# Twelve more tiles of a Trainium2 kernel's first input projection as products of rounded halves, with another order of the column blocks

## The chip, the cores and the metric

The kernel runs on 1 core of one Trainium2 chip. The metric is device microseconds of one execution; lower is better. Engines are called TensorE (PE in the profile, PEld for its weight loads), VectorE (DVE), ScalarE (ACT), GpSimd (POOL) and SyncE (SP, which issues nearly all DMAs).

## What is computed

Two layers, one after the other. The first is a hybrid block: the normalised stream u (272 positions, 1024 channels) is projected to q, f, i, g (1024 columns each, for 8 HGRN heads), z (1024), x, B, C (1536 together, with a causal convolution) and dt, for a Mamba-2 mixer of 16 heads. Both mixers' outputs go through w_out, and a gated feed-forward with convolution follows. The second layer has a retention mixer and 16 experts. The change is in the first input projection, `proj = u @ w_in`:

```python
u = rmsnorm(h, norm1_w[l])
proj = u @ w_in[l]
hg_q, hg_f, hg_i, hg_g, m2_z, m2_xbc, m2_dt = jnp.split(proj, PROJ_SPLITS, axis=-1)
out_a = hgrn2_mixer(hg_q, hg_f, hg_i, hg_g, lbs[l], hg_norm_w[l])
out_b = mamba2_mixer(m2_z, m2_xbc, m2_dt, m2_conv_w[l], m2_conv_b[l], m2_dt_bias[l],
                     m2_a_log[l], m2_d[l], m2_norm_w[l])
h = h + jnp.concatenate([out_a, out_b], axis=-1) @ w_out[l]
...
def hgrn2_mixer(q, f_pre, i_in, g, lb, norm_w):
    f = lb + (1.0 - lb) * jax.nn.sigmoid(f_pre)
    k = 1.0 - f
    ...
    return (o * jax.nn.silu(g.astype(f32))).astype(q.dtype)
```

## The kernel before

**Tiles and units.** The projection has 52 tiles j = 0 to 51 (NPROJ, and one for dt), each 128 output columns by 272 positions over 8 blocks of 128 inputs. Four tiles share one unit of weights of 2 MB in a slot of `ring`. `ORDER` (L434) lists which block of 512 columns each unit holds: blocks 0 and 1 are q, 2 and 3 f, 4 and 5 i, 6 and 7 g, 8 and 9 z, 10 to 12 x, B and C. Tile j is column block ORDER[j // 4], part j % 4. Blocks 1, 3, 5 and 7 belong to HGRN heads 4 to 7.

**Two kinds of tile.** A tile outside `SPLIT` is 8 float32 products of `ring` and `uT` (L980). A tile in `SPLIT` (L53) is made of three products for each of the 8 blocks (`split_products`, L725, the products at L740, L741 and L744): ScalarE rounds the tile's weights into the last ring slot (`round_weights`, L1443, the operation at L1450), which holds four tiles (HB); VectorE subtracts the rounded from the full weights in place (`in_rest`, L1853, the operation at L1858, semaphore in_lo). TensorE waits for in_lo of its tile. The stream u has been rounded and split the same way once; `uin` (L244) says where the halves lie: in places of `proj` that later tiles write, and at the end of `arena`.

**Order of work.** Each engine has its own loop over j, written out by hand, and its queue runs in that order. On TensorE the Mamba steps stand between and inside tiles 16 to 30: `m2_spread`, then VectorE's `m2_scores` with ScalarE's `m2_exp`, then `m2_heads`. From tile 32 on, HGRN head h stands at tiles 32 + 3h, 33 + 3h and 34 + 3h (`hgrn`):

- TensorE: `hg_turn(h)` (transposes at L895 and L897, 16 records of score products at L904, L906, L910) ahead of tile 32 + 3h, for h = 0 after the first half of tile 32; `hg_out(h)` (L917 to L920) ahead of the next tile; `hg_mean(h)` (L928) ahead of the third. hg_turn(h) waits for hg_staged(h) of VectorE.
- VectorE, at the first of the three: `hg_values(h)` (L2069, L2070), `hg_mask(h)` (L2077), `hg_states(h)` (L2083, L2084), `hg_cumulate(h + 1)` (scans L2046, L2050); at the second: `hg_gate(h)` (L2091), `hg_finish(h - 1)` (L2096), `hg_decay(h + 1)` (L2059 to L2064), which ends with hg_staged.
- ScalarE, at the first: `hg_keys(h)` (L1572), the logarithms and the inverse root, the square of hg_out, and `hg_exps(h + 1)` (L1555 to L1557); then it evicts the tile (L1439), as it evicts every tile, with Silu for q, g and z, Sigmoid for f and Copy for the rest.

proj_tiles counts evicted tiles. For heads 4 to 7 hg_cumulate waits for 32 of them, hg_decay for 40, hg_gate for 44. Head 0 is cumulated and decayed at j = 30 on VectorE, behind the last m2_outputs. A slot of `ring` is loaded again by SyncE (`stream`) when its unit's last tile is done. After the tiles come heads' rest, the output projection, the feed-forward and the second layer, whose experts are read through the same ring and slots in `arena`.

Of the kernel before, what the change touches and what calls it, by code (L numbers as in the profile page):

```python
# [23 lines left out]
P = 128  # L24
D = 1024
KT = D // P
META, SEQ = 16, 256
T = META + SEQ
# [18 lines left out]
WORDS = 23040  # L47
# [2 lines left out]
TQ, TF_, TI, TG, TZ, TX, TBM, TCM = 0, 8, 16, 24, 32, 40, 48, 50  # L50
NPROJ = 52

SPLIT = range(2, 28)  # L53


def par_rows():
# [95 lines left out]
def build(nc, a, out):  # L152
    with ExitStack() as ctx:
# [85 lines left out]
        prow = A.take(4, P)  # L239
        chan = A.take(2, T)[0:16]  # L240

        xin_lo = Arena(WORDS - 8 * T - 16).take(4, T)

        def uin(part, k):  # L244

            if part == 0:
                return proj[:, (TF_, TQ)[k // 4] + 4 + k % 4, :]
            return proj[:, TI + 4 + k, :] if k < 4 else xin_lo[:, k - 4, :]
        at = A.at + 5 * T
        normed = Arena(0).take(3, D)  # L250
        norm1 = Arena(at + 3 * P).take(8)
# [13 lines left out]

        hg_k, hg_lf, hg_sq = (proj[:, TBM + i, :] for i in range(1, 4))

        m2_t = Arena(WORDS - 8 * T - 16 + 4 * T).take(2, T)
        rows_at = at - 5 * T
        A = Arena(x_at)  # L270
        m2_x = A.take(3, 512)
# [3 lines left out]
        m2_seg = A.take(256)  # L275
        m2P2 = A.take(4, 16)[0:16]
        m2C = A.take(4, 144)
        assert A.at <= x_at + 3 * D + 4 * P
        A = Arena(WORDS - T - 16)
        m2_halves = A.take(1, T)[0:48, 0]  # L280
        m2_pick = A.take(1, 16)[0:48, 0]
        A = Arena((TG + 4) * T)
        m2_xe = A.take(2, 512)
        m2_S = A.take(2, 512)
        m2P0 = A.take(4, P)
        m2P1 = A.take(4, P)
        assert A.at <= TX * T

        def ch(row):

# [140 lines left out]
        w_in, w_ada = a["w_in"][0], a["w_ada_2"][0]  # L431


        ORDER = [10, 11, 12, 2, 0, 4, 6, 3, 1, 5, 7, 8, 9]  # L434
        u_in, u_ada = [], []

        def ada_unit():
# [265 lines left out]
        def _(pe):  # L703
# [182 lines left out]
            def hg_turn(h):  # L886

                b = h % 2
                pe.wait_ge(ev("hg_staged"), h + 1)
                if h:  # L890
                    pe.wait_ge(ev("hg_gated"), h)
                else:
                    pe.wait_ge(ev("m2_out"), 8)
                for w, (t0, n) in enumerate(WINDOWS):
                    pe.transpose(ps[0:n, 6, w * P:w * P + P], proj[:, TI + h, t0:t0 + n], ident)  # L895
                for w in range(2):
                    mm = pe.transpose(ps[:, 7, w * P:w * P + P], hg_D[:, b, 3, w * P:w * P + P], ident)  # L897
                mm.then_inc(ev("hg_turned"), 1)
                keys = [hg_K0[:, b], hg_D[:, b, 0, :], hg_D[:, b, 1, :], hg_D[:, b, 2, :]]
                for l in range(4):  # L900
                    q = hg_B[:, b, max(l - 1, 0), :]
                    for w in range(2):
                        s = slice(w * P, w * P + P)
                        pe.matmul(ps[:, 4 + l // 2, (l % 2) * 256 + w * P:(l % 2) * 256 + w * P + P], keys[l][:, s], q[:, s], start=True, stop=True)  # L904
                pe.wait_ge(ev("hg_v"), h + 1)
                pe.matmul(ps[0:16, 6, 384:400], hg_K0[:, b, 256:T], hg_B[:, b, 0, 256:T], start=True, stop=True).then_inc(ev("hg_scores"), 1)  # L906

                pe.wait_ge(ev("hg_ke"), h + 1)
                for w in range(2):
                    mm = pe.matmul(ps[:, 7, w * P:w * P + P], hg_ke[:, w, :], hg_v[:, w, :], start=True, stop=True)  # L910
                mm.then_inc(ev("hg_update"), 1)
# [906 lines left out]
        def _(dve):  # L1818
# [202 lines left out]

            def m2_gate(g):
                dve.wait_ge(ev("m2_out"), 8)
                dve.wait_ge(ev("proj_tiles"), 48 + 4 * g)
                z = proj[:, TZ + 4 * g:TZ + 4 * g + 4, :]
                tt(z, z, proj[:, TX + 4 * g:TX + 4 * g + 4, :], ALU.mult).then_inc(ev("m2_gated"), 1)

# [11 lines left out]

            def hg_cumulate(h):  # L2040
                b = h % 2
                dve.wait_ge(ev("proj_tiles"), 16 if h < 4 else 32)
                st(ts(hg_k, proj[:, h + TF_, :], noml[:, h:h + 1], oml[:, h:h + 1], ALU.mult, ALU.add))
                dve.wait_ge(ev("hg_log"), h + 1)
                for l in range(4):
# [9 lines left out]
            def hg_decay(h):  # L2055
                b = h % 2
                dve.wait_ge(ev("hg_exp"), h + 1)

                st(dve.tensor_copy(small[:, 120 + b:121 + b], hg_B[:, b, 3, 255:256]))  # L2059
                st(tt(hg_K0[:, b], hg_K0[:, b], hg_k, ALU.mult))  # L2060
                st(tt(hg_D[:, b], hg_D[:, b], hg_k[:, 0:256].unsqueeze(1).to_broadcast([P, 4, 256]), ALU.mult))
                st.wait()
                dve.wait_ge(ev("proj_tiles"), 24 if h < 4 else 40)
                st.link(tt(hg_B[:, b], hg_B[:, b], proj[:, h + TQ, :].unsqueeze(1).to_broadcast([P, 4, T]), ALU.mult))  # L2064
                dve.nop().then_inc(ev("hg_staged"), 1)

# [20 lines left out]
            def hg_gate(h):  # L2087

                dve.wait_ge(ev("hg_squared"), h + 1)
                dve.wait_ge(ev("proj_tiles"), 28 if h < 4 else 44)  # L2090
                stt(proj[:, h + TQ, :], ps[:, 6, 0:T], pc("hgn", h), proj[:, h + TG, :], ALU.mult, ALU.mult).then_inc(ev("hg_gated"), 1)  # L2091

            def hg_finish(h):
# [24 lines left out]

            for j in range(NPROJ):
                n, m = divmod(j, 4)  # L2120
                if j + 3 in SPLIT and j + 3 > SPLIT[1]:
                    in_rest(j + 3)
                if 1 <= j <= 12:
                    conv(j - 1)
# [23 lines left out]
                if j == 30:  # L2148
# [3 lines left out]
                    hg_cumulate(0)  # L2152
                    hg_decay(0)
                hgrn(j)
                if j == 48:
                    m2_gate(0)
            m2_gate(1)
# [373 lines left out]
```

## Time and profile before

| | us |
|---|---|
| median of 3 runs | 1646.63 (1646.13 to 1646.7) |
| profiled execution | 1646.37 |
| its span, first to last instruction | 1644.4 |

```profile
span 1644.4 us, 21062 instructions
PE 1302.6 (79%) x8468; PEld 780.6 (47%) x8468; DVE 501.7 (31%) x946; ACT 478.0 (29%) x725; POOL 254.9 (16%) x197
```

The second line gives each engine's busy time, its share of the span and its instructions. The page's second part cuts the span into 40 equal slices of 41 us; each digit is the busy share in tenths. A row of a timeline gives start, duration, engine, line, operation, and in square brackets the idle time of the engine before it with what ended it. Matmul records overlap, so the step between starts tells the rate, not the duration of one.

### The profile page before, as it was taken

How to read it: one execution, taken by the hardware profiler on the slowest of the kernel's cores; microseconds unless marked ns; L12 is line 12 of the kernel's file. 1: busy time of each engine (PE TensorE's matmuls, PEld its weight loads, DVE VectorE, ACT ScalarE, POOL GpSimd, SP SyncE). 2: the span in 40 equal slices, each digit the busy share in tenths (PEclk: the TensorE clock that was granted, in tenths of full speed). 3: DMA queues.
4: the chain of work that ended last, by engine and by line, in shares of the span. 5: the costliest groups of instructions: out<-in, count | busy, mean ns of one | idle time of the engine just before them, and what ended most of it. 6: DMA issues, size and time to landing. Idle time of an engine off the chain costs nothing.

```text
span 1644.4 us, 21062 instructions
## 1 busy us (share of the span) xinstructions
PE 1302.6 (79%) x8468; PEld 780.6 (47%) x8468; DVE 501.7 (31%) x946; ACT 478.0 (29%) x725; POOL 254.9 (16%) x197
## 2 busy tenths in 40 slices
PE   9999999999999999998656656665666666666575
PEld 8787888889999889662111111111111111111111
DVE  6775767256763725440000000000000000000001
ACT  7754566256564536531101101100110110010001
POOL 0000000149879645200000000000000000000000
PEclk9999999999999999989888889878878877878877
DMA  8955432277443823579999999999999999999997
GB/s 313 339 205 183 148 103 103 103 247 239 155 180 141 296 94 123 197 315 408 429 429 429 428 428 428 429 428 428 428 428 430 429 427 428 429 428 429 429 428 284
DMA packets 94081, 524.04 MB, mean 319 GB/s; under 512 B 8089, under 2 KB 32177, under 8 KB 66113
## 3 DMA queue, kind: packets, MB, share of 16 engines
q1 hardware_dynamic: 93681, 522.61, 78.5%
q8 instruction: 45, 0.74, 0.2%
q10 hardware_dynamic: 336, 0.54, 0.1%
q14 instruction: 19, 0.16, 0.0%
HBM read 522.08 MB, written 1.05 MB: 318 GB/s over the span
## 4 chain that ended last, share of the span: by engine, by line
DMA 47%; PE 43%; DVE 4%; SPq 3%; ACT 2%; issue 1%; DVEq 0%; ACTq 0%
DMA ring<-in_w_down 24%; DMA ring<-in_w_up 22%; PE ps L740 6%; PE ps L744 6%; PE ps L741 6%; PE ps L980 4%; PE ps L1353 4%; PE ps L1032 3%; PE ps L1377 3%; PE ps L1249 2%; SPq L558 2%; SPq L571 1%; PE ps L722 1%; PE ps L904 1%; PE ps L807 1%
## 5 line engine op out<-in xcount | busy, mean ns | idle before, releaser
L1353 PE MATMUL ps<-ring,arena 128*32 128x512 f32 x1984 | 288.1, 720 | 163.8 <-DMA ring<-in_w_up 121.2
L740 PE MATMUL ps<-arena_r,ring_r 128*128 128x258 f32 (+3 forms) x960 | 287.2, 299 | 2.1 <-DVE uT_r L2194 1.1
L744 PE MATMUL ps<-arena_r,ring_r 128*128 128x258 f32 (+3 forms) x960 | 280.0, 292 | 0.0
L1377 PE MATMUL ps<-ring,arena 128*32 128x512 f32 x944 | 163.3, 829 | 94.4 <-DMA ring<-in_w_down 87.6
L1353 PEld LDWEIGHTS ps<-ring,arena 128*32 128x32 f32 x1984 | 61.8, 121 | 359.2 <-DMA ring<-in_w_up 182.5
L1811 POOL TENSOR_TENSOR ring_r<-ring,ring_r 128x512 fp32r<-128x512 f32 (+1 forms) x96 | 128.6, 1339 | 419.9 <-ACT ring_r L1450 419.8
L740 PEld LDWEIGHTS ps<-arena_r,ring_r 128*128 128x128 f32 x960 | 181.9, 189 | 9.8 <-issue 6.1
L744 PEld LDWEIGHTS ps<-arena_r,ring_r 128*128 128x128 f32 x960 | 181.0, 188 | 2.9
L741 PE MATMUL ps<-arena_r,ring_r 128*128 128x256 f32 (+2 forms) x608 | 179.3, 295 | 0.0
L1814 POOL TENSOR_TENSOR arena<-arena 128x512 f32<-128x512 f32 x1 | 1.3, 1318 | 965.4 <-ACT arena L1796 965.4
L1450 ACT ACTIVATE ring_r<-ring 128x1024 fp32r<-128x1024 f32 (+1 forms) x122 | 126.4, 1038 | 36.8 <-PE ps L741 21.0
L1812 POOL TENSOR_TENSOR ring_r<-ring,ring_r 128x512 fp32r<-128x512 f32 (+1 forms) x96 | 131.2, 1367 | 0.0
L1377 PEld LDWEIGHTS ps<-ring,arena 128*32 128x32 f32 x944 | 30.5, 132 | 211.1 <-DMA ring<-in_w_down 153.0
L741 PEld LDWEIGHTS ps<-arena_r,ring_r 128*128 128x128 f32 x608 | 114.8, 189 | 4.3 <-issue 1.2
L980 PE MATMUL ps<-uT,ring 128*128 128x272 f32 x416 | 101.2, 396 | 0.0
L1770 ACT ACTIVATE arena<-ps 128x512 f32<-128x512 f32 x16 | 9.6, 597 | 312.1 <-PE ps L1364 312.1
L741 PE MATMUL ps<-uT_r,ring_r 128*128 128x258 f32 x352 | 99.5, 283 | 0.0
L2478 DVE TENSOR_TENSOR arena<-arena,ps 128x512 f32<-128x512 f32 x16 | 11.0, 688 | 283.5 <-PE ps L1353 283.5
L2482 DVE COPY arena<-ps 128x512 f32<-128x512 f32 x15 | 10.4, 692 | 274.3 <-PE ps L1377 274.3
L980 PEld LDWEIGHTS ps<-uT,ring 128*128 128x128 f32 x416 | 77.7, 191 | 15.8 <-issue 0.8
L1774 ACT ACTIVATE arena<-ps 128x512 f32<-128x512 f32 x15 | 9.0, 597 | 251.6 <-PE ps L1377 251.6
L1384 PE MATMUL ps<-arena 128*128 128x512 f32 x120 | 62.5, 668 | 13.6 <-DVE arena L2482 13.6
(414 smaller groups left out, 1519.9 us busy)
## 6 DMA issues: line engine op xcount, KB each, us to landing
ring<-in_w_gate SPq DMA_DIRECT2D x64, 2048.0 KB, 25.9
ring<-in_w_down SPq DMA_DIRECT2D x62, 2048.0 KB, 26.1
ring<-in_w_up SPq DMA_DIRECT2D x60, 2048.0 KB, 24.4
ring<-in_w_in SPq DMA_DIRECT2D x19, 2048.0 KB, 12.4
ring<-in_w_ada SPq DMA_DIRECT2D x12, 2048.0 KB, 11.6
ring<-in_ffn_w_up SPq DMA_DIRECT2D x22, 1024.0 KB, 7.9
ring<-in_w_out SPq DMA_DIRECT2D x6, 2048.0 KB, 7.8
ring<-in_ffn_w_down SPq DMA_DIRECT2D x4, 2048.0 KB, 8.0
```

The source lines that it names most:

```text
L558: sp.dma_start(dst, src, **kw).then_inc(ev(sem), 16)
L740: pe.matmul(o, hi[:, k, :], r_(xhi(k0 + k)), start=first and k == 0, stop=False)
L741: mm = pe.matmul(o, hi[:, k, :], r_(xlo(k0 + k)), start=False, stop=False)
L744: mm = pe.matmul(o, lo[:, k, :], r_(xhi(k0 + k)), start=False, stop=last and k == nk - 1)
L980: mm = pe.matmul(o[:, 0:T], w[:, k, :], uT[:, k, :], start=k == 0, stop=k == KT - 1)
L1032: mm = pe.matmul(o[:, 0:KEPT], kcols(u_out[cb][half], m)[:, i, :], x, start=first and n == 0, stop=last and n == len(blocks) - 1)
L1353: mm = pe.matmul(ps[32 * j:32 * j + 32, half, :], xs[:, kt, :], wk[:, 512 * j:512 * j + 512], start=kt == 0, stop=kt == KT - 1)
L1377: mm = pe.matmul(ps[32 * j:32 * j + 32, half, :], heT[:, j, 32 * i:32 * i + 32], wj[:, 512 * half:512 * half + 512], start=i == 0, stop=i ...
L1384: mm = pe.matmul(ps[:, 4 + b, :], Gt[:, w * P:w * P + P], ye[:, half * 512:half * 512 + 512], start=first, stop=False, skip_group_check=True)
L1450: act.activation(r_(rounded(c)), chunks[c][1], ACT.Copy).then_inc(ev("w_hi"), 1)
L1811: pool.tensor_tensor(r_(w[:, 0:mid, :]), w[:, 0:mid, :], hi[:, 0:mid, :], ALU.subtract).then_inc(ev("w_lo"), 1)
L1812: pool.tensor_tensor(r_(w[:, mid:, :]), w[:, mid:, :], hi[:, mid:, :], ALU.subtract).then_inc(ev("w_lo"), 1)
```

## The change

`SPLIT` takes in tiles 28 to 31 and eight of the tiles 32 to 43, two of every three (32, 33, 35, 36, 38, 39, 41, 42). The order of the column blocks moves block 8 (z) from tiles 44 to 47 to tiles 28 to 31, and blocks 3, 1, 5 and 7 each four tiles later. The rounded stream moves to the end of `arena` and the rest of the stream to places of z and g, and several Mamba buffers move to make room. Waits on proj_tiles follow the new order, hg_turn gets one, and hg_gate of head h from 4 on waits for 41 + h tiles. VectorE calls in_rest for tiles 32 and up behind hgrn(j), for tile j + 2; ScalarE rounds tile j + 3 at j, as before.

```diff
-SPLIT = range(2, 28)
+SPLIT = list(range(2, 32)) + [j for j in range(32, 44) if (j - 32) % 3 < 2]
...
-        xin_lo = Arena(WORDS - 8 * T - 16).take(4, T)
+        xin_hi = Arena(WORDS - 8 * T).take(8, T)
...
             if part == 0:
-                return proj[:, (TF_, TQ)[k // 4] + 4 + k % 4, :]
-            return proj[:, TI + 4 + k, :] if k < 4 else xin_lo[:, k - 4, :]
+                return xin_hi[:, k, :]
+            return proj[:, (TZ, TG)[k // 4] + 4 + k % 4, :]
...
-        m2_t = Arena(WORDS - 8 * T - 16 + 4 * T).take(2, T)
+        m2_t = proj[:, TQ + 4:TQ + 6, :]
...
-        A = Arena((TG + 4) * T)
-        m2_xe = A.take(2, 512)
-        m2_S = A.take(2, 512)
+        m2_xe = Arena((TQ + 4) * T).take(2, 512)
+        m2_S = Arena((TF_ + 4) * T).take(2, 512)
+        A = Arena((TI + 4) * T)
...
-        ORDER = [10, 11, 12, 2, 0, 4, 6, 3, 1, 5, 7, 8, 9]
+        ORDER = [10, 11, 12, 2, 0, 4, 6, 8, 3, 1, 5, 7, 9]
...
                 pe.wait_ge(ev("hg_staged"), h + 1)
+                pe.wait_ge(ev("proj_tiles"), 24 if h < 4 else 37 + h)
...
-                dve.wait_ge(ev("proj_tiles"), 48 + 4 * g)
+                dve.wait_ge(ev("proj_tiles"), 52 if g else 32)
...
-                dve.wait_ge(ev("proj_tiles"), 16 if h < 4 else 32)
+                dve.wait_ge(ev("proj_tiles"), 16 if h < 4 else 36)
...
-                dve.wait_ge(ev("proj_tiles"), 24 if h < 4 else 40)
+                dve.wait_ge(ev("proj_tiles"), 20 if h < 4 else 40)
...
-                dve.wait_ge(ev("proj_tiles"), 28 if h < 4 else 44)
+                dve.wait_ge(ev("proj_tiles"), 28 if h < 4 else 41 + h)
...
-                if j + 3 in SPLIT and j + 3 > SPLIT[1]:
+                if j + 3 in SPLIT and SPLIT[1] < j + 3 < 32:
                     in_rest(j + 3)
...
                 hgrn(j)
+                if 30 <= j < 42 and (j - 32) % 3:
+                    in_rest(j + 2)
```

## Rows read from the trace of the kernel before

**Rows 1.** Page, part 2: 40 slices, busy tenths of TensorE and of the DMA engines.

```profile
PE   9999999999999999998656656665666666666575
...
DMA  8955432277443823579999999999999999999997
```

**Rows 2.** Page, part 4: the chain that ended last, shares by line.

```profile
DMA ring<-in_w_down 24%; DMA ring<-in_w_up 22%; PE ps L740 6%; PE ps L744 6%; PE ps L741 6%; PE ps L980 4%; PE ps L1353 4%; PE ps L1032 3%; PE ps L1377 3%; PE ps L1249 2%; SPq L558 2%; SPq L571 1%; PE ps L722 1%; PE ps L904 1%; PE ps L807 1%
```

**Rows 3.** Windows: stretch, length, busy by engine, granted clock, DMA share, GB/s.

```profile
734.00:736.00 2.00, 1.70 (x20) 0.73 (x19) 0.33 (x2) 0.40 (x2) 0.00 (x0) 1.00 0.00 0
```

**Rows 4.** Waits, 96 to 290 us: engine and line, releaser, total, times, longest.

```profile
PE ps L910 <- ACT arena L1572: 0.7, 1, 0.7
PE ps L895 <- DVEq L2065: 0.6, 1, 0.6
...
DVE small L2059 <- ACT arena L1557: 13.9, 8, 2.6
```

**Rows 5.** Chain in order of time: start, length, what; one float32 tile.

```profile
185.01 3.67 PE ps L980 x16
```

**Rows 6.** Timeline of TensorE, two products of one split tile, 46 steps apart.

```profile
42.25 0.29 PE L741 MATMUL ps<-arena_r,ring_r 128*128 128x272 f32 x1
...
47.99 0.29 PE L744 MATMUL ps<-arena_r,ring_r 128*128 128x272 f32 x1
```

**Rows 7.** Groups by line and form, 0 to 300 us: count, busy us, mean ns.

```profile
L1858 DVE TENSOR_TENSOR ring_r<-ring,ring_r 128x1024 fp32r<-128x1024 f32 x26 | 31.7, 1222 | 17.1 <-ACT ring_r L1450 15.0 <-ACT arena L1532 1.5 <-DVE par L2133 0.2
...
L1450 ACT ACTIVATE ring_r<-ring 128x1024 fp32r<-128x1024 f32 x26 | 27.5, 1056 | 7.4 <-DMA ring<-in_w_in 5.2 <-ACT arena L1439 2.2
```

**Rows 8.** Timeline, tiles 29 to 32 and the staging of head 0.

```profile
152.15 0.20 PEld L879 LDWEIGHTS ps<-arena 128*64 128x64 f32 x4 [0.36 <-DVEq L2014]
...
155.19 0.61 ACT L1550 ACTIVATE arena<-arena,small 128x272 f32<-128x272 f32 x1 [1.14 <-DVE arena L2020]
...
163.93 2.10 PE L980 MATMUL ps<-uT,ring 128*128 128x272 f32 x8
164.29 1.29 DVE L2064 TENSOR_TENSOR arena<-arena 128x1088 f32<-128x1088 f32 x1
...
165.74 0.69 DVE L1895 COPY arena<-ps 128x512 f32<-128x512 f32 x1 [0.15 <-DVE arena L2064]
165.87 0.38 PE L895 MATMUL ps<-cst,arena 128*128 128x128 f32 x2
```

**Rows 9.** Timeline, from the staging of head 2 to the staging of head 3.

```profile
196.02 1.29 DVE L2064 TENSOR_TENSOR arena<-arena 128x1088 f32<-128x1088 f32 x1
...
197.71 0.49 PE L895 MATMUL ps<-cst,arena 128*128 128x128 f32 x3
...
198.80 0.27 DVE L2070 COPY arena<-ps 16x128 f32<-16x128 f32 x1
...
200.14 0.21 PE L906 MATMUL ps<-arena 128*16 128x16 f32 x2
...
200.39 1.88 DVE L2077 COPY_PREDICATED arena<-cst,ps 128x256 f32<-128x256 uint32 x4 [1.32 <-PE ps L906]
...
212.02 1.29 DVE L2064 TENSOR_TENSOR arena<-arena 128x1088 f32<-128x1088 f32 x1
```

**Rows 10.** Timeline, gate of head 4, decay of head 5, evictions after the exps.

```profile
239.90 0.50 DVE L2091 SCALAR_TENSOR_TENSOR arena<-ps,par,arena 128x272 f32<-128x272 f32 x1 [0.23 <-DVE arena L2050]
...
242.32 0.15 DVE L2059 COPY small<-arena 128x1 f32<-128x1 f32 x1 [1.56 <-ACT arena L1557]
...
243.60 0.91 ACT L1439 ACTIVATE arena<-ps 128x272 f32<-128x272 f32 x2
```

**Rows 11.** Windows around a gap of TensorE in the second layer.

```profile
787.00:788.00 1.00, 0.00 (x0) 0.00 (x0) 0.00 (x0) 0.00 (x0) 0.00 (x0) 1.00 0.84 360
...
790.00:791.00 1.00, 1.00 (x8) 0.00 (x0) 0.00 (x0) 0.00 (x0) 0.00 (x0) 0.50 0.88 377
```

**Rows 12.** Timeline of TensorE, the end of that gap.

```profile
788.59 2.56 PE L1353 MATMUL ps<-ring,arena 128*32 128x512 f32 x16 [2.48 <-DMA ring<-in_w_up]
```

More of the change, by code:

```diff
@@ L277, in build @@
         m2C = A.take(4, 144)
-        assert A.at <= x_at + 3 * D + 4 * P
-        A = Arena(WORDS - T - 16)
         m2_halves = A.take(1, T)[0:48, 0]
         m2_pick = A.take(1, 16)[0:48, 0]
-        A = Arena((TG + 4) * T)
-        m2_xe = A.take(2, 512)
-        m2_S = A.take(2, 512)
+        assert A.at <= x_at + 3 * D + 4 * P
+        m2_xe = Arena((TQ + 4) * T).take(2, 512)
+        m2_S = Arena((TF_ + 4) * T).take(2, 512)
+        A = Arena((TI + 4) * T)
         m2P0 = A.take(4, P)
         m2P1 = A.take(4, P)
-        assert A.at <= TX * T
         def ch(row):
```

## Prediction

> **What bounds the kernel now.** I read the page first, then the chain that ended last, then the waits and the timeline of the stage that is edited. The page's slices [rows 1] show two kernels in one: up to about slice 17 TensorE is at 9 of 10 and the DMA engines are half idle; from slice 18 on the DMA engines are full and TensorE half idle. In the chain [rows 2] the second part is expert weights (in_w_down 24%, in_w_up 22%) and the first is TensorE. The experts' stream is throttled by slots that TensorE frees, and just before its steady state the DMA engines stand still with all slots full [rows 3]. So it begins when TensorE arrives, and what the first part gains or loses moves the end one for one. The edited stage is 128 to 275 us, the later input projection tiles with the Mamba heads and then the HGRN heads between them. TensorE looks saturated there: from 96 to 290 us its two longest waits are 0.7 us for ScalarE and 0.6 us for the head's staging on VectorE, once each [rows 4]. That reading hides something: the other chain through that stage is almost exactly as long as TensorE's own work, so taking work from TensorE alone need not gain.
>
> **What a split tile saves on TensorE.** A plain float32 tile is 16 records and takes 3.67 us [rows 5]. A split tile is 24 records. From one L741 at 42.25 to an L744 at 47.99 there are 46 steps, so (47.99 - 42.25) / 46 = 0.125 us each [rows 6], and 24 of them are 3.00 us. The saving is 0.67 us a tile, 12 x 0.67 = 8.0 us if TensorE alone sets the time. In exchange each tile costs one rounding on ScalarE (1.06 us) and one subtraction on VectorE (1.22 us) [rows 7].
>
> **Tiles 28 to 31: nearly nothing.** From the fourth spread on, TensorE does half of tile 28 and tile 29, and then waits 0.36 us for the scores of VectorE before the Mamba heads at 152.15; after them come VectorE's outputs, ScalarE's logarithm at 155.19, the scans, ScalarE's exps, and at 164.29 the last product that stages head 0 (ends 165.58) [rows 8]. That chain is not shortened by quicker tiles: only the first half of tile 28 lies ahead of it, worth half of the 0.67, that is 0.33 us. Two new roundings of 1.06 us (tiles 32 and 33) come ahead of the logarithm on ScalarE in that stretch; I work them out to end just when it is due, and they eat the 0.33. So staging of head 0 still ends at about 165.6. The roundings for tiles 28 to 31 fall earlier, where VectorE waits for TensorE. The subtraction of tile 29 can delay the third scores by its own 1.22 us, which TensorE, coming to them late, covers; cover gone, 1.2 us. I take nothing.
>
> **Tile 32: a new wait of 2.8 us.** The loop of VectorE calls in_rest(32) at j = 30 behind hg_decay(0), in an in-order queue. Now TensorE starts the first half of tile 32 at 163.93 and the turn of head 0 at 165.87 [rows 8], and that half needs nothing from VectorE. In the changed kernel it needs the rest of tile 32's weights: VectorE takes it up at 165.74 (where it now takes up L1895), ends 1.22 later at 166.96, TensorE starts at about 167.05, needs 12 x 0.125 = 1.5 us and some 0.1 to go over, and turns head 0 at 168.65. That is 2.8 us later than 165.87. Queued behind tile 32 are head 0's transposes, and behind those everything in the loop. in_rest(33) and the copy of the ada row then run during this wait.
>
> **The loop over heads: two subtractions on the path.** Staging of head 2 ends at 196.02 + 1.29 = 197.31 and of head 3 at 212.02 + 1.29 = 213.31: a period of 16.0 us [rows 9]. Of it the stretch from the mask at 200.39 to 213.31 is 12.92 us and does not depend on projection tiles. If TensorE came at once it would turn 0.1 us after staging, do the scores 2.43 us later (197.71 to 200.14), and the mask starts 0.25 after: 0.1 + 2.43 + 0.25 + 12.92 = 15.7 us. So even free tiles could gain only 0.3 us per head. Now in_rest(j + 2) is called at j = 33 and 34, 36 and 37, 39 and 40: each pair sits between one head's staging and the same head's hg_values. In steps: 0.15 to take it up, 2 x 1.24 = 2.5, then L2069 and L2070 (0.34 and 0.27, the second from 198.80 to 199.07: 0.6), 0.1 to TensorE, then 0.25 to the mask and 12.92: 16.5 to 16.6. Against 16.0 each of three heads loses 0.57, together 1.7 us. ScalarE's roundings lie behind its exps or ahead of hg_keys, not inside the 12.92; if they grew past the keys they would cost up to 1.06 each.
>
> **The gate of head 4: 2.5 us, once.** The order moves G's upper block from tiles 40 to 43 to tiles 44 to 47. hg_gate(4) is called on VectorE at j = 45 and waits for 41 + 4 = 45 tiles, so for tile 44's eviction. On ScalarE that eviction stands behind hg_exps(5), and it needs a table load. Today the gate runs at 239.90 under the exps, with the finish behind it, and L2059 starts at 242.32 when the exps end; the evictions follow a table load, from 243.60 [rows 10]. In the changed kernel the gate can start at 243.6 + 0.4 + 0.25 = 244.25, gate and finish take some 0.8 together, and decay starts at 245.05: 2.73 later. Behind the waiting gate on VectorE is hg_decay(5), for which TensorE's next turn waits. Less the slack of 16.0 - 15.7, this costs 2.5 us (2.4 to 2.5). Heads 5 to 7 gate on tiles evicted long before, and the loop is TensorE's again: no recovery.
>
> **Other edits at nothing.** The tiles' new places in SBUF change no wait; the added wait of hg_turn is met (tile 40 is done four tiles ahead of head 4). F's upper block at 32 to 35 is needed at j = 41, Q's at j = 42, both ready. An extra table load between a sigmoid and a silu eviction (1.28 us) lies on ScalarE between exps and keys, in a gap of the same size; cover gone, it would cost up to 1.3 us. Z's block is earlier, but its gate is used at j = 48 as before, behind hg_decay(6).
>
> **Sum.** 2.8 + 1.7 + 2.5 = +7.0 us on the profiled execution of 1646.37 us (span 1644.4 and 2.0 around it). The median of the runs is 1646.63, 0.26 above. 1646.6 + 7.0 = **1653.6 us**, +0.43%.
>
> **Rivals.** (1) *TensorE is the bound all the way*: the page's 9s [rows 1] and the short waits speak for it; the times of [rows 8, 9] against it. All 8.0 us: 1638.6. That partly comes true, 1640 to 1643, if VectorE's new work slips into its gaps (it idles 13.9 us before L2059 [rows 4]) and the gate too; program order speaks against it. (2) *Only one of the waits bites*: tile 32's stall shortened since the stage before arrives early, or ScalarE evicting tile 44 sooner than I read. 1646.6 + 1.7 + 0 to 2.5: 1646.6 to 1650. (3) *The clock falls in the new gaps.* TensorE would idle for some 4.9 us ahead of tile 32 (it now starts it 3.1 earlier, after 0.8 of issue, and tiles 29 to 31 are 1 to 2 quicker), then 1.9 us per head. In the trace the granted clock is 1.00 (2.4 GHz) in 787 to 788, inside a gap of 2.48 us that ends at 788.59, and 0.50, the 1.2 GHz level, in 790 to 791 [rows 11, 12]. The gap ahead of tile 32 is longer than that one, those of the heads shorter, and the trace doesn't show which of them would do it. At half clock the half tile costs 3.0 for 1.5 and a turn and its scores 4.9 for 2.43: up to +4 us at head 0, up to +1.5 (0.9 of 2.4 is hidden under the subtractions) at each of three others. Time 1655 to 1660; likeliest 1656. The Trainium skill (TensorE: Matmul & The Clock Gate, Part 1) says that an idle stretch lets the gate pass half the pulses only, and [rows 11] agrees; by that rule alone tile 32's gap would bring this, and the sum would be about 1656. It speaks against the change: quicker tiles in front of a fixed chain are longer gaps. (4) *The change doesn't do what it says*: the tiles stay float32, but the waits remain; the counts of L740 and L980 would tell. I give it nothing.
>
> **How the numbers follow.** Forecast (1650 to 1655) 0.53; clock rival (1655 to 1660) 0.17; one wait only (1646.6 to 1650, two thirds of it within 0.2%) 0.14; gain of some size 0.11; other, slower still, 0.05. A measurement of this kernel can tell about 0.2%, or 3.3 us, from no change. So faster 0.10, same 0.11, slower 0.79. The range leaves out the gain and what is slower than 1660 together with a part of the second rival's low end: 1647.0 to 1659.0.
>
> **What would show it.** L980 down from 416 to 224 records, L740 from 960 to 1056. TensorE waiting for VectorE before tile 32's first L740, some 5 us; a wait on L2065 before L895 for each of heads 1 to 5 (1 to 2.6 us), none for heads 6 and 7; L2091 waiting on ScalarE L1439 once for about 4 us; turns at 168.7, 184.5, 201.0, 217.6, 234.1 and 252.7; from there everything about 7 us later. If turns 1 to 4 come 15.2 us apart or less, the chain was read wrong and rival 1 is right. If L2091 waits once but the turn does not, ScalarE evicted early.

## The result, and the profile after

The changed kernel takes 1654.05 us (median of 6 runs, 1651.87 to 1654.95) against 1647.04 (1646.13 to 1648.12) for the kernel before beside it: a ratio of 1.0045, with a 95% interval of 1.0035 to 1.0056. That is 7.0 us more; 1653.6 was forecast. The profiled execution is 1654.41 us against 1646.37, 8.0 more. The total came out as forecast, but in part because errors behind it cancel.

The page of the changed kernel, its span, engines and its group of split products (columns as in the page of before):

```profile
span 1652.3 us, 21299 instructions
...
PE 1301.2 (79%) x8564; PEld 782.4 (47%) x8564; DVE 515.2 (31%) x958; ACT 490.0 (30%) x737; POOL 255.1 (15%) x197
...
L738 PE MATMUL ps<-arena_r,ring_r 128*128 128x258 f32 (+3 forms) x1056 | 316.9, 300 | 6.5 <-DVE ring_r L1857 5.3
```

The tiles are split as the diff says: 1056 records of the split product (L738 now, L740 before). Grouped by line and form from 0 to 300 us, the float32 products (L979 now) are 224 and the subtractions 38 where [rows 7] has 26:

```profile
L979 PE MATMUL ps<-uT,ring 128*128 128x272 f32 x224 | 53.9, 394 | 0.4 <-DVE uT L1849 0.4
L1857 DVE TENSOR_TENSOR ring_r<-ring,ring_r 128x1024 fp32r<-128x1024 f32 x38 | 46.1, 1223 | 21.4 <-ACT ring_r L1449 18.7 <-ACT arena L1531 1.5 <-DVE arena L2063 0.6
```

The waits from 96 to 300 us (engine and line, what it waited for, total, times, longest). In [rows 4] TensorE's longest were 0.7 and 0.6, once each (L894 is the turn, L738 the first split product of tile 32, L2090 the gate); the three longest kinds that have come in all lie in or behind VectorE's queue:

```profile
PE ps L894 <- DVEq L2064: 5.7, 5, 2.1
...
PE ps L738 <- DVE ring_r L1857: 4.5, 1, 4.5
DVE arena L2090 <- ACTq L1625: 4.5, 1, 4.5
```

The timeline around tile 32 (start, duration; idle time in brackets). It answers to [rows 8], where tile 32's first half starts at 163.93 and head 0 is turned at 165.87:

```profile
164.13 1.29 DVE L2063 TENSOR_TENSOR arena<-arena 128x1088 f32<-128x1088 f32 x1
165.58 2.36 DVE L1857 TENSOR_TENSOR ring_r<-ring,ring_r 128x1024 fp32r<-128x1024 f32 x2 [0.15 <-DVE arena L2063]
...
166.95 0.56 PE L738 MATMUL ps<-arena_r,ring_r 128*128 128x272 f32 x1 [4.47 <-DVE ring_r L1857]
167.31 0.43 PE L739 MATMUL ps<-arena_r,ring_r 128*128 128x272 f32 x1
...
169.81 0.84 PE L894 MATMUL ps<-cst,arena 128*128 128x128 f32 x3
```

TensorE comes to tile 32 4.47 us early and starts at 166.95 (forecast: some 5 us, 167.05). Then it turns head 0 12 products later, 2.86 us where full clock gives 1.5. The windows of that stretch (length, TensorE busy, granted clock, DMA share, GB/s) say why:

```profile
165.00:166.00 1.00, 0.00 (x0) 1.00 1.06 414
166.00:167.00 1.00, 0.05 (x1) 0.54 1.04 406
167.00:168.00 1.00, 1.00 (x5) 0.50 1.05 395
172.00:173.00 1.00, 1.00 (x7) 0.55 0.98 360
173.00:174.00 1.00, 1.00 (x10) 1.00 0.07 25
```

A granted clock of 1.00 is 2.4 GHz and 0.50 is 1.2 GHz. Having done nothing since its last product, TensorE is granted 1.2 GHz from about 166 to 173. The second long wait is the gate of head 4, with [rows 10] as its counterpart (gate at 239.90 after 0.23 idle, no wait at the turn):

```profile
250.09 0.91 ACT L1438 ACTIVATE arena<-ps 128x272 f32<-128x272 f32 x2
250.63 0.50 DVE L2090 SCALAR_TENSOR_TENSOR arena<-ps,par,arena 128x272 f32<-128x272 f32 x1 [4.47 <-ACTq L1625]
...
254.47 0.61 PE L894 MATMUL ps<-cst,arena 128*128 128x128 f32 x3 [2.14 <-DVEq L2064]
...
255.30 3.35 PE L903 MATMUL ps<-arena 128*128 128x128 f32 x16
```

The gate waits 4.47 us for ScalarE's evictions, decay(5) runs behind it, and the turn of head 5 comes after 2.14 us of idle TensorE. The clock falls only after TensorE has started again (0.91 from 254 to 255). The 16 score products then take 3.35 us, at a granted clock of 0.50 from 255 to 258; at full clock they take 1.95 (head 1 of this kernel, and the runs below).

Where each head's turn (its first transpose: L895 before, L894 after) stands, in us, and the time from one to the next:

| | head 0 | 1 | 2 | 3 | 4 | 5 | 6 | 7 |
|---|---|---|---|---|---|---|---|---|
| before | 165.87 | 181.67 | 197.71 | 213.70 | 229.69 | 245.68 | 261.67 | 281.86 |
| forecast | 168.7 | 184.5 | 201.0 | 217.6 | 234.1 | 252.7 | | |
| after | 169.81 | 187.10 | 203.44 | 219.77 | 236.12 | 254.47 | 272.14 | 292.33 |
| step, before | | 15.80 | 16.04 | 15.99 | 15.99 | 15.99 | 15.99 | 20.19 |
| step, after | | 17.29 | 16.34 | 16.33 | 16.35 | 18.35 | 17.67 | 20.19 |

The loop ends 10.5 us late; the forecast had 7.0. From there the gap shrinks. A line of products at the end of the first layer (32 records on `cond`, L807 before and L805 now) starts at 340.96 before and 351.42 after, still 10.5 apart; the router's first product starts at 734.44 and 743.18, 8.7 apart; the last group of expert products at 1625.70 and 1633.55, 7.9 apart.

### The profile page after: what moved, and what is told of

It reads as the page before. It is cut to its first block, busy times and chain, and to the rows that moved or that the text cites. A ratio compares the mean times of both kernels' runs of the same rounds, so it can differ in the third digit from the quotient of the medians.

```text
span 1652.3 us, 21299 instructions
## 1 busy us (share of the span) xinstructions
PE 1301.2 (79%) x8564; PEld 782.4 (47%) x8564; DVE 515.2 (31%) x958; ACT 490.0 (30%) x737; POOL 255.1 (15%) x197
## 4 chain that ended last, share of the span: by engine, by line
DMA 47%; PE 38%; DVE 8%; ACT 3%; SPq 3%; issue 1%; DVEq 0%; ACTq 0%
DMA ring<-in_w_down 24%; DMA ring<-in_w_up 22%; PE ps L738 6%; PE ps L742 6%; PE ps L739 6%; PE ps L1352 4%; PE ps L1031 3%; PE ps L1376 3%; PE ps L1248 2%; SPq L556 1%; DVE arena L2045 1%; SPq L569 1%; DVE ring_r L1857 1%; PE ps L720 1%; DVE arena L2076 1%
## 5 line engine op out<-in xcount | busy, mean ns | idle before, releaser
L738 PE MATMUL ps<-arena_r,ring_r 128*128 128x258 f32 (+3 forms) x1056 | 316.9, 300 | 6.5 <-DVE ring_r L1857 5.3
L742 PE MATMUL ps<-arena_r,ring_r 128*128 128x258 f32 (+3 forms) x1056 | 308.8, 292 | 0.0
L739 PE MATMUL ps<-arena_r,ring_r 128*128 128x256 f32 (+2 forms) x704 | 207.8, 295 | 0.0
L738 PEld LDWEIGHTS ps<-arena_r,ring_r 128*128 128x128 f32 x1056 | 200.5, 190 | 15.3 <-issue 11.5
L742 PEld LDWEIGHTS ps<-arena_r,ring_r 128*128 128x128 f32 x1056 | 199.7, 189 | 2.9
L1449 ACT ACTIVATE ring_r<-ring 128x1024 fp32r<-128x1024 f32 (+1 forms) x134 | 139.1, 1040 | 39.2 <-PE ps L739 20.5
L739 PEld LDWEIGHTS ps<-arena_r,ring_r 128*128 128x128 f32 x704 | 133.6, 190 | 4.3 <-issue 1.2
L1769 ACT ACTIVATE arena<-ps 128x512 f32<-128x512 f32 x16 | 9.6, 597 | 311.9 <-PE ps L1363 311.9
L1773 ACT ACTIVATE arena<-ps 128x512 f32<-128x512 f32 x15 | 9.0, 597 | 251.6 <-PE ps L1376 251.6
L739 PEld LDWEIGHTS ps<-uT_r,ring_r 128*128 128x128 f32 x352 | 66.8, 190 | 0.0
L1767 ACT ACTIVATE arena<-ps 128x512 f32<-128x512 f32 x16 | 9.6, 597 | 163.4 <-PE ps L1352 163.4
```

Of the source, the lines that this page charges most:

```text
L738: pe.matmul(o, hi[:, k, :], r_(xhi(k0 + k)), start=first and k == 0, stop=False)
L739: mm = pe.matmul(o, hi[:, k, :], r_(xlo(k0 + k)), start=False, stop=False)
L742: mm = pe.matmul(o, lo[:, k, :], r_(xhi(k0 + k)), start=False, stop=last and k == nk - 1)
L1449: act.activation(r_(rounded(c)), chunks[c][1], ACT.Copy).then_inc(ev("w_hi"), 1)
```

## The experiments

Each edit is to the changed kernel unless said otherwise. "Loop end" is the turn of head 7 against 281.86 before. The timed ratio is against the kernel before on the same chip, with its 95% interval; 0.001 is 1.65 us. Turns and steps are read from one profile of each kernel.

**e1: the order, the places and the waits alone, with the old split.**

```diff
-SPLIT = list(range(2, 32)) + [j for j in range(32, 44) if (j - 32) % 3 < 2]
+SPLIT = list(range(2, 28))
...
-                if 30 <= j < 42 and (j - 32) % 3:
+                if j + 2 in SPLIT and 30 <= j < 42 and (j - 32) % 3:
```

> The changed kernel with its new order, places and waits, but the twelve added tiles stay float32 (SPLIT is 2 to 27). Theory: the gate of head 4 still waits for tile 44's eviction, so one period (turn of head 4 to turn of head 5) is 18.4 us instead of 16.0, and the clock may fall in that gap as in the changed kernel (+1.7): 2.4 to 4.1 us above before, less what is given back later: 1648.5 to 1651. Turns of heads 0 to 4 as before within 0.2 us. Rival (order costs nothing, all loss is from the split tiles): 1647.0.

Measured: steps of 15.80, 16.04, 15.99, 15.99, 18.28, 16.04; loop end +3.0; ratio 1.0019 (1.0010 to 1.0028), 3.1 us. Of the 3.0, 2.3 lie at the gate of head 4, the forecast's third term (2.5), and 0.7 at the start, where this profile is late already (it comes to the products ahead of tile 32 at 162.75, before at 162.07). TensorE waits 2.13 us before head 5's turn, nearly as long as the 2.14 of the changed kernel, and the clock stays up. Its windows (length, TensorE busy, granted clock, DMA share, GB/s):

```profile
246.00:247.00 1.00, 0.51 (x3) 1.00 0.00 0
247.00:248.00 1.00, 0.00 (x0) 1.00 0.00 0
248.00:249.00 1.00, 0.36 (x3) 1.00 0.00 0
249.00:250.00 1.00, 1.00 (x11) 1.00 0.00 0
```

**e2: e1 with tiles 28 to 31 split too.**

```diff
-SPLIT = list(range(2, 32)) + [j for j in range(32, 44) if (j - 32) % 3 < 2]
+SPLIT = list(range(2, 32))
...
-                if 30 <= j < 42 and (j - 32) % 3:
+                if j + 2 in SPLIT and 30 <= j < 42 and (j - 32) % 3:
```

> As the order-only kernel, but tiles 28 to 31 are split too (SPLIT is 2 to 31); tiles 32 up stay float32. Theory: the four tiles are hidden behind the scores and the staging of head 0, so the same time as the order-only kernel within 0.7 us. Rival (TensorE is the bound): 4 x 0.67 = 2.7 us less than order only.

Measured: loop end +2.4, 0.6 less than e1; ratio 1.0011 (1.0002 to 1.0020), 0.6 us less than e1 by the medians (1648.01, 1648.58). On TensorE these four tiles are 2.7 us less work. In e2 TensorE waits 0.95 us for the staging of head 0, where in e1 it does not wait. That 2.1 of the 2.7 vanish is what the forecast said, a chain that they don't lie on; the intervals of e1 and e2 overlap, so the 0.6 itself is not settled.

**e3: the subtractions of tiles 32 and 33 ahead of head 0's decay**, in the time in which VectorE waits for ScalarE's exps.

```diff
                     hg_cumulate(0)
+                    in_rest(32)
+                    in_rest(33)
...
-                if 30 <= j < 42 and (j - 32) % 3:
+                if 33 <= j < 42 and (j - 32) % 3:
```

> The changed kernel with in_rest(32) and in_rest(33) called between hg_cumulate(0) and hg_decay(0), where VectorE waits 2.65 us for ScalarE's exps. Theory: the wait of 4.5 us ahead of tile 32 is gone, head 0 turns at 165.6 instead of 169.8, the clock stays at 1.00 there, head 0's period is 15.8 instead of 17.3: up to 5.7 us less than the changed kernel, 1648.4; 1650 if a part of a shift is given back later anyway. Rival (most of the loss is the two subtractions per head and the gate): at most 1 us less, 1653.

Measured: turn of head 0 at 167.55, steps 15.86, 16.35, 16.33, 16.34, 18.35, 16.04; loop end +5.2; ratio 1.0019 (1.0010 to 1.0028). The subtractions cost the decay nothing; it starts when the exps are done (they run from 163.33 for 1.11 us):

```profile
161.98 2.36 DVE L1857 TENSOR_TENSOR ring_r<-ring,ring_r 128x1024 fp32r<-128x1024 f32 x2 [0.15 <-DVE arena L2049]
...
164.47 0.15 DVE L2058 COPY small<-arena 128x1 f32<-128x1 f32 x1
```

The wait ahead of tile 32 is gone, the clock stays up at heads 0 and 5, and head 0's step is 15.86. All of head 0's loss but the 1.7 of its turn goes; in this one profile the exps of head 0 end at 164.47, where those of the changed kernel end 2.0 us earlier, and that covers the 1.7. The two kernels run the same program up to there, and the first Mamba spread already starts at 95.05 in e3 and 93.06 in the changed kernel: the start of this stage differs that much from one profile to another.

**e4: the gate of head 4 behind the decay of head 5.**

```diff
+                    if h == 4:
+                        hg_decay(h + 1)
                     hg_gate(h)
...
-                    if h + 1 < HEADS:
+                    if h + 1 < HEADS and h != 4:
```

> The changed kernel with hg_decay(5) ahead of hg_gate(4) and hg_finish(3) on VectorE, for that head alone. Theory: the turn of head 5 no longer waits for tile 44's eviction but only for the gate behind the staging (0.5 us): period 16.3 instead of 18.35, and no fall of the clock behind it (1.7 us): 2 to 3.7 us less than the changed kernel, 1650.3 to 1652. Rival (the gate is covered): the same as the changed kernel.

Measured: step of head 4 16.52 instead of 18.35, of head 5 16.02 instead of 17.67; loop end +6.9, 3.6 less than the changed kernel; ratio 1.0033 (1.0021 to 1.0045). The clock still falls ahead of tile 32, where the wait is 4.47 again (head 0's step 16.90), and does not fall at head 5, whose gap of 2.14 us has gone. What is left there is a wait of 0.31 us for the gate of head 4, since the turn of a head waits for the gate of the head before it as well as for its own staging.

**e5: TensorE kept busy in its two gaps**, by 9 products of 272 columns ahead of tile 32 and 4 ahead of head 5's turn, whose results are overwritten unread.

```diff
+                if j == 47:
+                    early_o = open_tile("p47")
+                    for k in range(4):
+                        pe.matmul(early_o[:, 0:T], ident, uT[:, k, :], start=True, stop=True)
...
+                if j == 32:
+                    for k in range(9):
+                        pe.matmul(o[:, 0:T], ident, uT[:, k % KT, :], start=True, stop=True)
```

> The changed kernel with products that nobody reads on TensorE in its two longest gaps: nine of 272 columns into tile 32's own bank ahead of its wait for in_rest(32), four into tile 47's bank ahead of the turn of head 5. The results are overwritten. Theory (the half clock behind those gaps is part of the loss): the clock stays at 1.00, head 0's turn comes 1.2 us earlier behind in_rest(32), its period is 15.8 instead of 17.3 and head 5's 16.0 instead of 17.7: 4.3 us less than the changed kernel, though the waits themselves stay. Rival (the clock is covered by VectorE's chain): the same as the changed kernel within 0.5 us.

Measured: the half tile takes 1.57 us (167.65 to 169.22) instead of 2.86, head 0's step is 15.81 instead of 17.29, head 5's 16.04 instead of 17.67. Nothing else changes (16.32, 16.33, 16.34, 18.35). The timeline:

```profile
163.11 4.39 PE L967 MATMUL ps<-uT,cst 128*128 128x272 f32 x18
167.65 0.36 PE L738 MATMUL ps<-arena_r,ring_r 128*128 128x272 f32 x1
...
169.22 0.49 PE L894 MATMUL ps<-cst,arena 128*128 128x128 f32 x3
...
169.77 1.95 PE L903 MATMUL ps<-arena 128*128 128x128 f32 x16
```

Against the changed kernel that is 1.3 + 1.5 + 1.6 = 4.4: so 4.4 us of the 10.5 in the changed kernel's profile are the clock's, and adding useless work to TensorE takes them away. The loop end is +6.7, 3.7 less than the changed kernel's, because this profile comes to tile 32 0.7 late. Ratio 1.0030 (1.0018 to 1.0041) against 1.0045: 2.5 us less than the change, where 4.3 were expected and the profile has 3.6 less (1650.83 against 1654.41). The intervals of the two ratios overlap by 0.0006, so in the time the clock's share is less certain than in the profile.

**e6: each pair of subtractions apart**, one behind the finish of the previous head, where VectorE waits for the exps, one behind hg_values. Tiles 32 and 33 stay where the change has them.

```diff
+                    if j + 1 in SPLIT and j >= 35:
+                        in_rest(j + 1)
                     hg_mask(h)
...
+                    if j + 2 in SPLIT:
+                        in_rest(j + 2)
                     if h + 1 < HEADS:
                         hg_decay(h + 1)
...
-                if 30 <= j < 42 and (j - 32) % 3:
+                if j == 30 or j == 31:
```

> The changed kernel with the two subtractions per head moved: in_rest(35 + 3h) ahead of hg_decay(h + 1), where VectorE waits 1.6 us for the exps, and in_rest(36 + 3h) between hg_values(h + 1) and hg_mask(h + 1), where it waits 1.3 us for the scores; 32 and 33 stay. Theory: turns of heads 1 to 4 come 15.7 to 15.8 us apart instead of 16.34, TensorE waiting a bit less than 1.1 us for each: 1.7 to 1.9 us less than the changed kernel. Rival (the chain is ScalarE's, with its roundings): periods unchanged.

Measured: steps of heads 1 to 3 15.78, 15.78, 15.77 instead of 16.34, 16.33, 16.35. The pair between staging and values is what cost them, and once it is out of the way the step is what the forecast had worked out for free tiles, 15.7. The waits ahead of tile 32 (4.47) and head 5 (2.14) stay and the clock falls at both (steps 16.56 and 17.57); loop end +8.3; ratio 1.0037 (1.0023 to 1.0051).

**e7: e3, e4 and e6 together.**

> All three: in_rest(32) and (33) ahead of hg_decay(0), the pairs in the gaps, hg_decay(5) ahead of hg_gate(4). Theory: the three places hold the whole loss; head 0 turns when it does before, heads 1 to 4 turn 15.75 us apart, head 5 16.2 to 16.5 later: loop end 0.5 to 1 us ahead of before, time 1644.5 to 1646.5 where before is 1645.5 to 1647: 0 to 1 us faster than before, though TensorE has 8.0 us less work. Rival (TensorE is the bound once the stalls are gone): 8 us faster than before.

Measured: steps 15.86, 15.78, 15.76, 15.76, 16.53, 16.01, 20.20; loop end 0.02 from before; ratio 0.9998 (0.9989 to 1.0007). The three places hold the whole loss. And TensorE, with 8 us less work up to there, is no faster. Its longest waits, 96 to 290 us (all of them come to 7.6 us, before to 1.6):

```profile
PE ps L894 <- DVEq L2064: 4.4, 4, 1.4
PE ps L909 <- ACT arena L1571: 1.7, 2, 0.9
```

**e8: the kernel before again**, as one of the kernels compared, to see how far two profiles of one kernel differ.

> The kernel before once more, for a second profile. Its first profile had the clock at 0.57 from 720 to 730 us and 393.5 us from the eighth ada unit to the first router product, where five other profiles have 391.8 to 392.1. Theory (that is where in a window the clock falls, by chance): this profile has 391.9 as well, and its time is that of before. Rival (it belongs to the kernel): 393.5 again.

Measured: every turn within 0.1 us of before (loop end -0.07), ratio 1.0002 (0.9993 to 1.0011). But the stretch from the 32 records on `cond` to the router took 395.22 us, neither the 391.9 of the theory nor the 393.5 of the rival (before took 393.48): a difference as large as what the changed kernel seemed to give back there. The section on the hardware takes this up.

**e9: the kernel before with 26 products of 272 columns ahead of tile 32**, results unread: a pure delay with TensorE busy.

```diff
+                if j == 32:
+                    for k in range(26):
+                        pe.matmul(o[:, 0:T], ident, uT[:, k % KT, :], start=True, stop=True)
```

> The kernel before with 26 products that nobody reads (26 x 0.458 = 11.9 us) into tile 32's bank ahead of tile 32: a pure delay of the loop with the clock kept up. Theory (the first part moves the end one for one): 11.9 us above before, 1657.5 to 1658. Rival (about a quarter of a delay in the loop is given back in the second layer, as the single profiles so far look: 10.5 at the loop's end, 7.0 to 8.0 in the time): 9 us above, 1655.

Measured: turn of head 0 at 177.98, steps as before; loop end +12.1, the last expert products +12.7; ratio 1.0068 (1.0055 to 1.0081), 11.2 us with an interval of 9.1 to 13.3, and 12.25 by the medians. A delay in this loop passes to the end one for one, as the forecast took from the DMA engines standing still in [rows 3]. That three quarters of it would pass, 9.0, lies just outside.

**e10: e4, with the subtractions of tiles 32 and up on GpSimd.**

```diff
+                    pool.wait_ge(ev("w_hi"), c + 1)
+                    pool.tensor_tensor(r_(w), w, f_(rounded(c)), ALU.subtract).then_inc(ev("w_lo"), 1)
...
-                if 30 <= j < 42 and (j - 32) % 3:
-                    in_rest(j + 2)
```

> The changed kernel with the subtractions of tiles 32 up on GpSimd, which is idle there, and with hg_decay(5) ahead of hg_gate(4). Theory: VectorE's chain is freed of them and is the floor again: no wait ahead of tile 32, turns of heads 1 to 4 15.75 us apart, loop end as with all three moved, time 0 to 1 us below before. Rival (two engines on one memory slow each other): VectorE's operations longer where GpSimd runs, periods of 16.3 or more.

Measured: steps 15.87, 15.79, 15.79, 15.78, 16.54, 16.01; loop end +1.0, all of it there at head 0 already. Ratio 1.0015 (1.0007 to 1.0024), 2.5 us, with a median of 1648.68 (1644.13 to 1652.98), though its profiled execution was its quickest, 1644.13. From head 1 on the loop did what was expected. Head 0 is the rival's case: the operation ahead of its scans (L2048) takes 1.88 us where it takes 0.42 in e7, and ends just behind GpSimd's two subtractions of that stretch, which delays the exps and the staging. The time is 1.5 us over the loop's 1.0, and why stays open. The timeline of VectorE and GpSimd:

```profile
152.33 4.71 POOL L1812 TENSOR_TENSOR ring_r<-ring,ring_r 128x1024 fp32r<-128x1024 f32 x2 [151.88 <-ACT ring_r L1451]
155.32 1.88 DVE L2048 TENSOR_SCALAR arena<-arena,small 128x272 f32<-128x272 f32 x1
...
166.87 0.55 PE L896 MATMUL ps<-cst,arena 128*128 128x128 f32 x3 [2.75 <-DVEq L2070]
...
182.66 4.71 POOL L1812 TENSOR_TENSOR ring_r<-ring,ring_r 128x1024 fp32r<-128x1024 f32 x2 [13.02 <-ACT ring_r L1451]
...
185.47 1.91 DVE L2082 COPY_PREDICATED arena<-cst,ps 128x256 f32<-128x256 uint32 x4 [1.32 <-PE ps L907]
```

**e11: e10 with the head's chain shortened.** ScalarE reports the first two of its three exps, and VectorE's first two decay products start then instead of after the third.

```diff
+                act.nop().then_inc(ev("hg_exp"), 1)
...
-                dve.wait_ge(ev("hg_exp"), h + 1)
-                st(dve.tensor_copy(small[:, 120 + b:121 + b], hg_B[:, b, 3, 255:256]))
+                dve.wait_ge(ev("hg_exp"), 2 * h + 1)
...
+                dve.wait_ge(ev("hg_exp"), 2 * h + 2)
+                st(dve.tensor_copy(small[:, 120 + b:121 + b], hg_B[:, b, 3, 255:256]))
```

> As the last, and VectorE starts hg_decay's first two products when ScalarE has done the exps of K0 and D, not behind the one of B (1.11 us); the copy of the chunk decay goes behind B. Theory (the loop's floor is the chain from mask through cumulate, exps and decay to the turn, 15.7 us): the chain is 1.1 us shorter, turns of heads 0 to 4 come 14.65 to 14.9 us apart, which is TensorE's own work; loop end 5 to 6 us ahead of before: 1640 to 1641.5. Rival (another chain is as long): periods stay at 15.7, 1645.5.

Measured: steps 14.79, 15.54, 16.11, 14.70, 15.99, 15.99, 19.78; loop end -2.8; ratio 0.9966 (0.9954 to 0.9978), 5.6 us faster than before (4.9 by the medians). Expected were steps of 14.65 to 14.9 and a loop end 5 to 6 ahead. The steps of heads 1 and 2 are longer: in each TensorE waits for ScalarE's keys (0.71 and 1.34 us), a second chain that the expectation did not have.

**e12: e7 with the same shorter chain**, the subtractions on VectorE.

> The kernel with all three moved, its subtractions on VectorE, with the same early start of hg_decay. Theory: VectorE's own work now fills the period (the subtraction ahead of the decay no longer fits into a gap): periods 15.2 to 15.4, loop end 2 to 3 us ahead of before, 1643 to 1644.5. Rival: as with GpSimd, 1641.

Measured: steps 15.00, 15.31, 16.32, 14.71, 15.98, 15.99, 19.78; loop end -3.5, last expert products -4.5, profiled execution -4.5; 1640.67 us (1639.28 to 1643.32), ratio 0.9961 (0.9948 to 0.9974), the fastest of all, 6.4 us under before (5.9 by the medians), where 1643 to 1644.5 was expected. Of the first four steps, expected at 15.2 to 15.4, two are shorter, one is as expected and one is longer; the profile also comes to tile 32 0.5 earlier than that of e7. The timeline shows the first decay products (L2058, L2059) under ScalarE's third exps (L1557):

```profile
207.69 1.11 ACT L1557 ACTIVATE arena<-arena 128x1088 f32<-128x1088 f32 x1
...
208.23 0.43 DVE L2058 TENSOR_TENSOR arena<-arena 128x272 f32<-128x272 f32 x1
...
208.58 1.22 DVE L2059 TENSOR_TENSOR arena<-arena 128x1024 f32<-128x1024 f32 x1
```

Only now do the split tiles pay. The step from head 3 to head 4, without a wait of TensorE at either end, is 14.71 against 15.99: 0.64 us for each of its two split tiles, where the forecast had 0.67. The eight in the loop are 5.4 us less work for TensorE by the forecast's price; the loop ends 3.5 early. The shorter chain was not run on the kernel before, without the new split tiles. There TensorE waits for a head's staging only once, 0.59 us, so most of the 5.9 us should need both; that is argued and not shown. One step, from head 2 to head 3, is longer than before (16.32 against 15.99): TensorE waits there for ScalarE's keys. The same in the timeline of e12:

```profile
195.99 1.28 ACT L1438 ACT_TABLE_LOAD   x1
...
198.40 1.06 ACT L1449 ACTIVATE ring_r<-ring 128x1024 fp32r<-128x1024 f32 x1 [0.19 <-ACT arena L1438]
199.36 0.36 ACT L1572 ACTIVATE arena<-ps 128x256 f32<-128x256 f32 x1
...
199.78 0.71 PE L909 MATMUL ps<-arena 128*128 128x128 f32 x4 [1.54 <-ACT arena L1572]
```

That is the extra table load between a sigmoid and a silu eviction, with two evictions and a rounding behind it and ahead of the keys: the forecast costed it at nothing with "cover gone, up to 1.3 us". With the chain shortened, the cover is gone. Whether the subtractions are better on GpSimd (e11) or on VectorE (e12) is not settled; the intervals overlap.

## Why the forecast was right, and where not

**Where the time goes.** It was right that TensorE's 9s in [rows 1] hide a second chain of equal length, and this carried the sign. e7 shows it: 8 us off TensorE and no change in time. e11 and e12 shorten the other chain, and then the time falls.

**What a split tile saves: 0.67 us.** Right: e12 shows 0.64. The 46 steps from 42.25 to 47.99 are those of two tiles of 24 records, not of one as [rows 6] is headed; the 0.125 us a step stand.

**Tiles 28 to 31: nearly nothing.** Right within 0.6 us (e2 against e1).

**Tile 32: 2.8 us.** The wait is right: 4.47 us, start at 166.95 against 167.05. The turn came at 169.81 instead of 168.65. In e5, where the same wait exists and TensorE is kept busy, the half tile takes 1.57 instead of 2.86. So of the 3.9 us at head 0 some 2.6 are the wait and 1.3 the clock.

**The loop: 0.57 for each of three heads.** Right in mechanism (e6), too large in size. Measured 0.30, 0.34 and 0.36, together 1.0 instead of 1.7. The step that failed is "2 x 1.24 = 2.5" plus 0.15 and 0.6 in a row: the timeline of the changed kernel shows the two subtractions take 2.36 together, and the first copy of the values starts before their recorded end:

```profile
187.10 0.55 PE L894 MATMUL ps<-cst,arena 128*128 128x128 f32 x3 [1.40 <-DVEq L2064]
187.14 2.36 DVE L1857 TENSOR_TENSOR ring_r<-ring,ring_r 128x1024 fp32r<-128x1024 f32 x2 [0.16 <-DVE arena L2063]
...
189.42 0.42 DVE L2068 COPY arena<-ps 128x256 f32<-128x256 f32 x1
...
190.13 0.21 PE L905 MATMUL ps<-arena 128*16 128x16 f32 x2 [0.48 <-DVEq L2071]
```

From the start of the pair to the first copy are 2.28 us, where the forecast had 2.5; the rest of its chain is as it had it. A chain of records on one engine is summed by the steps between starts, not by durations.

**The gate of head 4: 2.5 us, once.** Right: the step is 18.35 where the rows gave 16.0 + 2.5, so 2.4. e1 shows it alone (18.28), e4 takes it away (16.52).

**"No recovery" behind it, heads 5 to 7 as before.** Wrong for head 5: 17.67 instead of 15.99, since the clock fell behind its gap of 2.14 us (1.7 us).

**The clock, which was a rival with a chance of 0.17.** It came true in place, and was weighed too low. Its bound for head 0 was 4 us; measured are 1.3 + 1.5 = 2.8. It had up to 1.5 at each of three others; heads 1 to 4, with gaps of 1.40, 0.86, 0.43 and 0.87 us where the forecast had 1.9, show none, and head 5, which it did not name, shows 1.7. Together 4.4 to 4.5 us. The forecast had in hand the gap of some 4.9 us and [rows 11], where the clock fell around a shorter one of 2.48; that row gave more reason for the clock to fall than for it to stay up. The Trainium skill (TensorE: Matmul & The Clock Gate, Part 1) has it that an idle stretch brings the half rate, and tile 32 agrees; e1, at full clock after 2.13 us, shows that not every gap does.

**The sum.** In the profile, loop: 2.6 (wait at tile 32) + 1.0 (pairs) + 2.4 (gate) + 4.5 (clock) = 10.5, as measured. Then 1.7 us come back ahead of the router and 0.9 among the experts, so the profiled execution is 8.0 over before; the medians are 7.0 apart. The forecast left out 4.5 of clock and 2.6 of return, and put the pairs 0.7 too high. Its 7.0 is near the truth because these errors cancel: each of the three waits was found and sized, the rest was luck. The 7.0 between the medians is that of six executions each; how far the clock fell in those without a profile is not known. With the clock in the sum the forecast would have been nearer to the loop and farther from the time: the rival's own 1655 to 1660 begins above the 1654.05.

**One for one to the end.** Held for the pure delay (e9). The 1.7 us come from another place: see below.

## What to carry to other kernels

An engine that is busy 9 tenths can still share the bound with a second chain of the same length; write out that chain's period from one head's staging to the next before crediting work taken off the busy engine, and shorten the chain first (e12) or the work removed buys only gaps. Work added to an in-order queue costs nothing or everything by its place: the same eight subtractions and one gate cost the loop 10.5 us, with the clock that falls behind them, or none, by where they stand in VectorE's order (e7). Putting them on an idle GpSimd is not free of VectorE either (e10, head 0). Where an edit opens a gap ahead of TensorE of the size of one at which the trace already shows the clock falling, work out the slower products with the sum.

## What the runs showed of the hardware

**The clock after a gap.** A gap of 4.47 us was followed by 1.2 GHz in all three kernels that have it (changed, e4, e6). The fall did not end at one place: it made the half tile 2.85 or 2.86 us in all three, and the step of head 0 17.29, 16.90 and 16.56, against 15.81 at full clock, so its price was 2.8, 2.4 and 2.0 us. A gap of 2.1 us ahead of head 5 was followed by 1.2 GHz in the changed kernel and e6, and not in e1, e2 and e3, which have the same gap (2.13, 2.14, 2.14) and a granted clock of 1.00 throughout. A gap of 2.75 us ahead of head 0 in e10 was not followed by it either, where one of 2.48 was in [rows 11, 12]: the length of the gap alone does not decide. In the changed kernel and e6 the clock had fallen once before, at tile 32; in e1, e2 and e3 it had not. Whether the earlier fall matters, or where the gap lies in time, was not tried. Filling both gaps with products kept the clock up (e5).

**Time comes back where the clock falls less, before the router.** The stretch from the 32 records on `cond` to the router holds one or two falls of the clock in every profile, of different lengths. Two windows of it (length, TensorE busy, granted clock, DMA share, GB/s) in the kernel before:

```profile
680.00:705.00 25.00, 22.98 (x73) 1.00 0.84 343
720.00:745.00 25.00, 23.97 (x183) 0.80 0.60 240
```

The same two windows of the changed kernel:

```profile
680.00:705.00 25.00, 22.73 (x124) 1.00 0.46 179
720.00:745.00 25.00, 23.75 (x159) 0.86 0.82 332
```

And of e8, the kernel before again:

```profile
680.00:705.00 25.00, 22.99 (x70) 0.93 0.85 347
720.00:745.00 25.00, 23.46 (x175) 0.80 0.59 236
```

The clock takes 25 x (0.00 + 0.20) = 5.0 us from TensorE before, 25 x 0.14 = 3.5 after, and 25 x (0.07 + 0.20) = 6.8 in e8. The stretch takes 393.48, 391.76 and 395.22 us. Elsewhere in the stretch the granted clock is 1.00 in all three. Less the clock's share these are 388.5, 388.3 and 388.5: the same. So the 1.7 us given back are a shorter fall of the clock, and the same kernel shows 1.7 more or less from one profile to the next. In e6, e7, e11 and e12, which have the new order of blocks, the stretch takes 393.2 to 393.5, as before; in e1 to e5 391.8 to 392.1; in e9, which has the old order, 393.6, and in e10 391.1. So it does not go with the order. What decides the length of the fall was not found, nor where the 0.9 comes from that follows it: from the router to the last expert products before, e8 and e9 take 891.2 to 891.8, all the others 890.1 to 890.9.

**GpSimd beside VectorE.** One subtraction of 128x1024 takes 2.36 us on GpSimd against 1.22 on VectorE. Of VectorE's work beside it the mask's four copies are hardly slower (1.91 us against 1.88 in [rows 9]). The TENSOR_SCALAR operation ahead of the scans (128x272) is slower: 1.88 us in e10 and in e11 at head 0, and 0.64 at a later head of e11, where it takes 0.42 alone. All three times it ends 0.16 us behind the end of GpSimd's subtraction (157.20 and 157.04 in e10). In e10 this is why head 0 turns 0.9 us later than in e7.
